# Two of the four column chunks of the output projection as a block of seven products

## The chip, the core and the metric

The kernel runs on one core of a Trainium2 chip. A core has TensorE (PE, matrix products), VectorE (DVE) and ScalarE (ACT) for elementwise work, GpSimd (POOL), SyncE (SP, which issues most transfers) and 16 DMA engines. The metric is the device time of one launch in microseconds; the kernel before takes 2113.49 us, the median of three runs.

## What is computed

One decoder layer for 256 rows of width 2048, in float32: a SwiGLU feed-forward block, a token mixer (block-sparse attention and a convolution in parallel, merged by gates), a second feed-forward block, and a layer norm behind each. The change concerns the end of the mixer:

```
def token_mixer(h, w_in, ..., w_attn_out, w_out):
    ...
    merged = jax.nn.sigmoid(ga) * y_attn + jax.nn.sigmoid(gc) * y_conv
    return merged @ w_out                      # 256 x 2048 by 2048 x 2048
...
    h = layer_norm(DN_ALPHA * h + mix, ln2_g[l], ln2_b[l])
```

## The kernel before

**Arithmetic.** A float32 product is made of three PE products of a faster type: each factor is split into a high part (a rounded copy, made by ACT) and a low part (the rest, made by DVE), and hi x hi, hi x lo and lo x hi are summed in a bank of the accumulator. For a block of weights that means: a transfer lands it, ACT writes the high part, DVE the low part, then PE multiplies. A weight in this chain is either a *unit* (128x1024, half a megabyte, names raw, w_hi, w_lo, lines 767, 1315 and 2197 to 2199) or a *group* (128x2048, one megabyte: four blocks of 128 rows by 512 columns; names g_raw, g_hi, g_lo, lines 817, 1338 and 2259 to 2261).

**Where each way is used.** The feed-forward blocks and the mixer's input projection use groups. For pairs of column chunks, U and G, they use seven products instead of eight (Strassen's scheme in Winograd's form): the 256 x K factor is cut into four blocks (two row tiles, two halves of K), sums S1 to S4 of these are formed once (line 1540), and for each pair of chunks sums T1 to T4 of weight groups take the place of some of the weights. Such a sum is made by DVE (line 1346) or by a transfer from HBM that adds onto what lies in SBUF, which POOL issues (line 2102). The results share four banks X, Y, Z, W; what two results have in common is copied from bank to bank by ACT (fork, line 899).

**The output projection before** uses units: four column chunks of 512, each with 8 units of 2 blocks. A loop over chunks (rows_out) does for each chunk the units 0 to 3 for row tile 0, the same for row tile 1, then units 4 to 7 likewise; DVE adds each finished tile to the residual rows (line 1570) and takes the statistics for the norm (lines 1660, 1663). The last chunk does all of row tile 0 first, so that the norm of tile 0 (lines 1570 to 1605) runs beside PE's work on tile 1. The factor is the merged rows, turned by PE (turn_merged, line 2245) and split into oT_hi and oT_lo. Ahead of it stands the convolution's output projection, behind it the norm and the second feed-forward block.

**What sets the order.** Everything is written out by hand. Each engine runs its own list in order, and an instruction that waits holds back all behind it. Loads are issued by SP in one list; a load into a slot of g_raw waits until the low part of the slot's former content is made. Groups go round a ring of four split buffers (RING), so a split on ACT also waits until PE has used the group four places earlier.

## Time and profile before

| | |
|---|---|
| median of the runs (three: 2112.50 to 2113.76 us) | 2113.49 us |
| span of the profiled execution | 2109.5 us |
| PE busy, matmuls and transposes | 2095.7 us (99%), 9386 |
| DVE busy | 1877.2 us (89%) |
| ACT busy | 1402.9 us (67%) |
| POOL busy | 216.7 us (10%) |
| output projection, in the span | 1339.1 to 1427.9 us |

The span is the time from the first to the last instruction of the one profiled execution; the runs' times lie 4.0 us above it. All positions below are microseconds from the span's start. The busy time of PE counts each matmul by its length in the pipeline, with overlaps merged; the pace of PE is the distance between starts.

### The profile page before, as it was taken

How to read it: one execution, taken by the hardware profiler on the slowest of the kernel's cores; microseconds unless marked ns; L12 is line 12 of the kernel's file. 1: busy time of each engine (PE TensorE's matmuls, PEld its weight loads, DVE VectorE, ACT ScalarE, POOL GpSimd, SP SyncE). 2: the span in 40 equal slices, each digit the busy share in tenths (PEclk: the TensorE clock that was granted, in tenths of full speed). 3: DMA queues.
4: the chain of work that ended last, by engine and by line, in shares of the span. 5: the costliest groups of instructions: out<-in, count | busy, mean ns of one | idle time of the engine just before them, and what ended most of it. 6: DMA issues, size and time to landing. Idle time of an engine off the chain costs nothing.

```text
span 2109.5 us, 23778 instructions
## 1 busy us (share of the span) xinstructions
PE 2095.7 (99%) x9386; PEld 1734.6 (82%) x9386; DVE 1877.2 (89%) x1420; ACT 1402.9 (67%) x1313; POOL 216.7 (10%) x345
## 2 busy tenths in 40 slices
PE   9999999999999999999999999999999999999998
PEld 7888888888888888888888888888888888888886
DVE  7899999999996889999999986659899999999996
ACT  6677777777775546766676445335677777777773
POOL 0111111101110001011100000000111111100110
PEclk9999999999999999999999999999999999999999
DMA  9798988888985759998898556755788988899892
GB/s 369 253 295 260 279 270 266 291 300 277 289 279 231 276 158 311 299 269 270 304 301 262 212 185 240 260 178 200 244 294 255 282 272 267 290 302 278 288 285 113
DMA packets 92397, 556.65 MB, mean 264 GB/s; under 512 B 13056, under 2 KB 13440, under 8 KB 35200
## 3 DMA queue, kind: packets, MB, share of 16 engines
q1 hardware_dynamic: 68544, 437.69, 54.7%
q0 software_dynamic: 23744, 117.46, 25.8%
q8 instruction: 74, 1.21, 0.2%
q14 instruction: 35, 0.29, 0.0%
HBM read 534.13 MB, written 20.97 MB: 263 GB/s over the span
## 4 chain that ended last, share of the span: by engine, by line
PE 88%; DVE 8%; DMA 2%; ACT 1%; issue 1%; SPq 0%; DVEq 0%; ACTq 0%
PE acc L2259 14%; PE acc L2261 14%; PE acc L2260 14%; PE tb L2259 12%; PE tb L2261 12%; PE tb L2260 12%; PE acc L2197 3%; PE acc L2199 3%; PE acc L2198 3%; DVE g_lo L1338 3%; DVE cacc L1777 3%; DMA g_raw<-in_groups 1%; PE tb L2245 1%; DVE w_lo L1315 1%; DVE g_raw L1346 1%
## 5 line engine op out<-in xcount | busy, mean ns | idle before, releaser
L1338 DVE TENSOR_TENSOR g_lo<-g_raw,g_hi 128x2048 fp32r<-128x2048 f32 x506 | 1147.6, 2286 | 120.4 <-ACT g_hi L817 119.8
L817 ACT ACTIVATE g_hi<-g_raw 128x2048 fp32r<-128x2048 f32 x506 | 964.4, 1916 | 319.8 <-DVE g_raw L1346 121.5
L2259 PE MATMUL acc<-g_hi,xF_hi 128*128 128x512 f32 x1184 | 464.3, 392 | 0.6 <-ACT acc L899 0.6
L2261 PE MATMUL acc<-g_hi,xF_lo 128*128 128x512 f32 x1184 | 461.1, 389 | 0.0
L2260 PE MATMUL acc<-g_lo,xF_hi 128*128 128x512 f32 x1184 | 460.7, 389 | 0.0
L2259 PE MATMUL tb<-g_hi,xF_hi 128*128 128x512 f32 x760 | 296.3, 390 | 0.3 <-DVE g_lo L1338 0.2
L2261 PE MATMUL tb<-g_hi,xF_lo 128*128 128x512 f32 x760 | 295.7, 389 | 0.0
L2260 PE MATMUL tb<-g_lo,xF_hi 128*128 128x512 f32 x760 | 295.7, 389 | 0.0
L1346 DVE TENSOR_TENSOR g_raw<-g_raw,g_raw 128x2048 f32<-128x2048 f32 x120 | 274.3, 2286 | 1.3
L2259 PEld LDWEIGHTS acc<-g_hi,xF_hi 128*128 128x128 f32 x1184 | 222.3, 188 | 46.8 <-ACT acc L899 1.0
L2261 PEld LDWEIGHTS acc<-g_hi,xF_lo 128*128 128x128 f32 x1184 | 222.2, 188 | 46.8
L2260 PEld LDWEIGHTS acc<-g_lo,xF_hi 128*128 128x128 f32 x1184 | 222.4, 188 | 45.1
L2259 PEld LDWEIGHTS tb<-g_hi,xF_hi 128*128 128x128 f32 x760 | 142.7, 188 | 30.4 <-issue 1.1
L2261 PEld LDWEIGHTS tb<-g_hi,xF_lo 128*128 128x128 f32 x760 | 142.6, 188 | 29.8
L2102 POOL DMA_DIRECT2D g_raw<-in_groups x80 | 72.5, 941 | 918.8 <-DVE g_lo L1338 870.6
L2260 PEld LDWEIGHTS tb<-g_lo,xF_hi 128*128 128x128 f32 x760 | 142.7, 188 | 29.4
L767 ACT ACTIVATE w_hi<-raw 128x1024 fp32r<-128x1024 f32 x80 | 84.7, 1062 | 105.0 <-DMA raw<-in_stream 65.4
L2259 PE MATMUL tb<-g_hi,hT_hi 128*128 128x512 f32 x384 | 149.8, 390 | 0.0
L2261 PE MATMUL tb<-g_hi,hT_lo 128*128 128x512 f32 x384 | 149.4, 389 | 0.0
L2260 PE MATMUL tb<-g_lo,hT_hi 128*128 128x512 f32 x384 | 149.4, 389 | 0.0
L2259 PE MATMUL acc<-g_hi,hT_hi 128*128 128x512 f32 x320 | 124.7, 390 | 0.0
L2261 PE MATMUL acc<-g_hi,hT_lo 128*128 128x512 f32 x320 | 124.5, 389 | 0.0
(180 smaller groups left out, 2307.7 us busy)
## 6 DMA issues: line engine op xcount, KB each, us to landing
g_raw<-in_groups SPq DMA_DIRECT2D x356, 1024.0 KB, 7.2
g_raw<-in_groups POOLq DMA_DIRECT2D x80, 1024.0 KB, 8.6
raw<-in_stream SPq DMA_DIRECT2D x80, 512.0 KB, 4.5
bounce<-h_sq POOLq DMA_DIRECT2D x40, 256.0 KB, 5.5
h_in<-bounce POOLq DMA_DIRECT2D x160, 64.0 KB, 2.6
ln_gb<-in_ln SPq DMA_DIRECT2D x6, 1024.0 KB, 6.6
g_raw<-in_groups SPq DMA_DIRECT2D x6, 512.0 KB, 9.7
res<-in_x_rows SPq DMA_DIRECT2D x1, 2048.0 KB, 16.6
```

Of the source, the lines that this page charges most:

```text
L767: act.activation(w_hi[:, seg.split(j)], raw[:, seg.raw(j)], ACT.Copy).then_inc(hi_ready, 1)
L817: act.activation(g_hi[:, n % RING], source[:], ACT.Copy).then_inc(g_hi_ready, 1)
L1338: dve.tensor_tensor(g_lo[:, n % RING], source[:], f32(g_hi[:, n % RING]), ALU.subtract).then_inc(g_lo_ready, 1)
L1346: dve.tensor_tensor(out[:], a[:], b[:], ALU.add).then_inc(t_ready, 1)
L1777: ins = dve.scalar_tensor_tensor(out=rows if j == TAPS - 1 else cacc[:, k], in0=rows, scalar=w, in1=cacc[:, k], op0=ALU.mult, op1=ALU.add)
L2102: pool.dma_start(out=source(f, b, onto)[:].rearrange("p k n -> p (k n)"), in_=groups[k], accum_op=ALU.add).then_inc(ready, 16)
L2197: pe.matmul(out_ap, x[0][:, k, rows], w_hi[:, s, cols], start=begin, stop=False)
L2198: pe.matmul(out_ap, x[0][:, k, rows], w_lo[:, s, cols], start=False, stop=False)
L2199: return pe.matmul(out_ap, x[1][:, k, rows], w_hi[:, s, cols], start=False, stop=end)
L2259: pe.matmul(bank, x_hi_ap, g_hi[:, n % RING, blk], start=begin, stop=False, skip_group_check=True)
L2260: pe.matmul(bank, x_hi_ap, g_lo[:, n % RING, blk], start=False, stop=False, skip_group_check=True)
L2261: return pe.matmul(bank, x_lo_ap, g_hi[:, n % RING, blk], start=False, stop=end, skip_group_check=True)
```

## The change

The weights of the output projection are loaded as groups. Column chunks 0 and 3 stay plain (groups a0 to a3 and b0 to b3). Chunks 1 (U) and 2 (G) become one block of seven products P1 to P7, each in two halves a and b of four matmul blocks. Its loads are qa, qb, ga, gb (chunk G) and ra, rb, ua, ub (chunk U). PE's order is the table OUT: P1a and P1b stand between a1 and a2. Six of the eight sums of weights are made by accumulating transfers (T1: q + r, T3: r + u, T4: q + g, for a and b), two by DVE (T2: q + u). The four factor sums are made by DVE and split by ACT and DVE. The loads of the norm's constants and of the second feed-forward block's first groups move behind the block's loads in SP's list, and SP's slots for these change. Core of the diff:

```diff
+OUT = ("a0", "a1", "P1a", "P1b", "a2", "a3", "P2a", "P2b", "P5a", "P5b", "P6a", "P3a", "P6b", "P3b", "P7a", "P7b", "P4a", "P4b",
+       "b0", "b1", "b2", "b3")
+OUT_LOADS = {"a0": "a0", "a1": "a1", "qa": "P4a", "qb": "P4b", "a2": "a2", "ra": "P7a", "rb": "P7b", "a3": "a3", "ga": "P2a",
+             "gb": "P2b", "ua": "P3a", "ub": "P3b", "b0": "b0", "b1": "b1", "b2": "b2", "b3": "b3"}
+OUT_SUMS = ("T2a", "T2b")
+OUT_FACTORS = (S1, S2, S4, S3)
+OUT_PLAIN = (0, 3)
+OUT_U, OUT_G = 1, 2
...
-            load_once(mix_out)
-
-            for j in range(mix_out.n):
-                load(mix_out, 1, j)
-            sp.wait_ge(tr_full, t_ln2)
+            slot_free(KO, 4)
+            load_group(KO)
+            sp.wait_ge(tr_full, t_convt + 4)
+            load_group(KO + 1)
+            load_group(KO + 2)
+            sp.wait_ge(lo_ready, UNITS - 2)
+            load_group(KO + 3)
+            sp.wait_ge(lo_ready, UNITS)
+            load_group(KO + 4)
+            for k in range(KO + 5, K1):
+                if k in G.behind_conv:
+                    sp.wait_ge(unit_used, UNITS)
+                load_group(k)
+            sp.wait_ge(g_used, G.at["out", 0, "P7b"] + 1)
             load_gb(1, ln_gb[1])
-            for k in range(K1, K1 + 2):
+            for k in range(K1, K2):
+                if k in G.behind_out:
+                    sp.wait_ge(g_used, N1)
                 load_group(k)
-            loads(mix_out, 2)
-            sp.wait_ge(unit_used, mix_out.unit(ND - 1, 0))
-            sp.wait_ge(lo_ready, mix_out.unit(ND - 1, UD))
-            for k in range(K1 + 2, K1 + 4):
-                load_group(k)
-            sp.wait_ge(unit_used, mix_out.unit(ND - 1, UD))
-            load_ffn(1, K1 + 4, K2)
...
+            def out_pair():
+
+                f, g = "out", 0
+                split_out("a2")
+                out_factor_hi(0)
+                split_out("a3")
+                out_factor_hi(1)
+                fork(f, g, acc[:, BY], acc[:, BX], "P1b")
+                split_loaded(f, g, "P2a", "ga")
+                out_factor_hi(2)
+                split_loaded(f, g, "P2b", "gb")
+                out_factor_hi(3)
+                act.wait_ge(t1a_ready, 16)
+                split(f, g, "P5a", "qa")
+                act.wait_ge(t1b_ready, fulls(f, g) - 16 * NG)
+                split(f, g, "P5b", "qb")
+                split_sum(f, g, "P6a", "qa", "T2a")
+                split_loaded(f, g, "P3a", "ua")
+                split_sum(f, g, "P6b", "qb", "T2b")
+                act.wait_ge(acc_out[1], 2 * (u1_end + 1))
+                fork(f, g, acc[:, BZ], acc[:, BW], "P5b")
+                split_loaded(f, g, "P3b", "ub")
+                act.wait_ge(t3a_ready, 16 * BLOCKS)
+                split(f, g, "P7a", "ra")
+                act.wait_ge(t3b_ready, fulls(f, g))
+                split(f, g, "P7b", "rb")
+                save_out(0, "P6b")
+                act.wait_ge(t4a_ready, fulls(f, g))
+                split(f, g, "P4a", "qa")
+                act.wait_ge(t4b_ready, 16 * (BLOCKS + 1))
+                split(f, g, "P4b", "qb")
+                save_out(1, "P7b")
...
+            def plain_rows(m, t):
+
+                if m and t == 0:
+                    dve.wait_ge(out_full, 1)
+                else:
+                    dve.wait_ge(g_used, G.at["out", 0, ("a3", "b3")[m]] + 1)
+                cols = slice(OUT_PLAIN[m] * COLS, (OUT_PLAIN[m] + 1) * COLS)
+                dve.scalar_tensor_tensor(out=res[:, t, cols], in0=res[:, t, cols], scalar=ALPHA, in1=acc[:, 2 + t],
+                                         op0=ALU.mult, op1=ALU.add).then_inc(acc_out[1], 1)
...
+            def out_pair():
+
+                f, g = "out", 0
+                qa, qb, ua, ub = (source(f, g, name) for name in ("qa", "qb", "ua", "ub"))
+                lo_group(f, g, "P1b", "qb")
+                out_factor_sum(0)
+                lo_out("a2")
+                out_factor_sum(1)
+                lo_out("a3")
+                out_factor_sum(2)
+                out_factor_lo(0)
+                lo_group(f, g, "P2a", "ga")
+                out_factor_lo(1)
+                out_factor_sum(3)
+                lo_group(f, g, "P2b", "gb")
+                out_factor_lo(2)
+                lo_group(f, g, "P5a", "qa")
+                load_done(f, g, "ua")
+                split_done(f, g, "P5a")
+                add(qa, qa, ua)
+                plain_rows(0, 0)
+                plain_rows(0, 1)
+                lo_group(f, g, "P5b", "qb")
+                lo_group(f, g, "P6a", "qa")
+                load_done(f, g, "ub")
+                split_done(f, g, "P5b")
+                add(qb, qb, ub)
+                lo_group(f, g, "P3a", "ua")
+                lo_group(f, g, "P6b", "qb")
+                out_factor_lo(3)
+                lo_group(f, g, "P3b", "ub")
+                lo_group(f, g, "P7a", "ra")
+                lo_group(f, g, "P7b", "rb")
+                g_rows(0)
+                lo_group(f, g, "P4a", "qa")
+                u_rows(0)
+                lo_group(f, g, "P4b", "qb")
+                u_rows(1)
...
+            out_pair()
+            lo_out("b0")
+            for t in range(TT):
+                plain_stats(0, t)
+            lo_out("b1")
+            g_rows(1)
+            lo_out("b2")
+            for n, t, c in ((1, 0, OUT_G), (2, 0, OUT_U), (3, 1, OUT_U)):
+                pair_stats(n, t, c)
+            lo_out("b3")
+            pair_stats(4, 1, OUT_G)
...
+            def out_sums():
+
+                f, g = "out", 0
+                pool.wait_ge(g_lo_ready, lo_count(G.at[f, g, "P1a"]))
+                add_from_hbm(f, g, "qa", "ra", t1a_ready)
+                pool.wait_ge(g_lo_ready, lo_count(G.at[f, g, "P1b"]))
+                add_from_hbm(f, g, "qb", "rb", t1b_ready)
+                for name, onto, ready in (("ra", "ua", t3a_ready), ("rb", "ub", t3b_ready)):
+                    k = G.load_at[f, g, name]
+                    pool.wait_ge(g_loaded[slot_of[k]], 16 * (slot_count[k] - sum(slot_of[h] == slot_of[k] for h in range(PARTED))))
+                    add_from_hbm(f, g, name, onto, ready)
+                pool.wait_ge(g_lo_ready, lo_count(G.at[f, g, "P6a"]))
+                add_from_hbm(f, g, "qa", "ga", t4a_ready)
+                pool.wait_ge(g_lo_ready, lo_count(G.at[f, g, "P6b"]))
+                add_from_hbm(f, g, "qb", "gb", t4b_ready)
+
+            out_sums()
...
+            def out_pair():
+
+                f, g = "out", 0
+                X, Y, Z, W = (acc[:, bank] for bank in (BX, BY, BZ, BW))
+                made = 7 + 4 * factors(f)
+                pe.wait_ge(lhs_lo, b_merge + 4)
+                out_plain(0, 0, True, False)
+                out_plain(1, 0, False, False)
+                turn_merged(ND - 1)
+                out_plain(0, 1, True, False)
+                out_plain(1, 1, False, False)
+                pe.wait_ge(acc_out[0], 2 * u0_mix)
+                out_product("P1a", X, A11, 0, begin=True)
+                out_product("P1b", X, A11, 1)
+                pe.wait_ge(lhs_lo, b_ln2)
+                for t in range(TT):
+                    out_plain(2, t, False, False)
+                    out_plain(3, t, False, True)
+                wait_fork(f, g, 0)
+                out_product("P2a", Y, A12, 0)
+                out_product("P2b", Y, A12, 1)
+                pe.wait_ge(x_lo, made + 1)
+                pe.wait_ge(acc_out[1], 2 * (u1_end + 1))
+                out_product("P5a", W, S1, 0, begin=True)
+                out_product("P5b", W, S1, 1)
+                pe.wait_ge(x_lo, made + 2)
+                out_product("P6a", X, S2, 0)
+                wait_fork(f, g, 1)
+                pe.wait_ge(x_lo, made + 3)
+                out_product("P3a", Z, S4, 0)
+                out_product("P6b", X, S2, 1)
+                out_product("P3b", Z, S4, 1)
+                wait_fork(f, g, 2)
+                pe.wait_ge(x_lo, made + 4)
+                out_product("P7a", X, S3, 0)
+                out_product("P7b", X, S3, 1)
+                wait_fork(f, g, 3)
+                out_product("P4a", X, A22, 0)
+                out_product("P4b", X, A22, 1)
...
+            def last_out():
+
+                n = G.at["out", 0, "b0"]
+                pe.wait_ge(out_rows, 1 + TT)
+                for t in range(TT):
+                    for p in range(PIECES):
+                        if t == 0:
+                            wait_lo(pe, n + p)
+                        hi_part, lo_part = out_piece(p, t)
+                        for blk in range(GK):
+                            mm = mm3(acc[:, 2 + t], hi_part[:, blk], lo_part[:, blk], n + p, blk, p == 0 and blk == 0,
+                                     p == PIECES - 1 and blk == GK - 1)
+                        if t == 1:
+                            mm.then_inc(g_used, 1)
+                            if p >= 2:
+                                turn_piece(p - 2, 10, b_ln2)
+                        elif p == PIECES - 1:
+                            mm.then_inc(out_full, 1)
...
```

In the rows below, g_raw_6N is slot N of g_raw (g_raw_70 is slot 10), acc is one of the four banks, and each row is one instruction or a repeated one, with the semaphores it waits for.

DVE, the output projection. Before, the rows ahead of the loop over chunks (w_lo is a unit's low part, oT_lo the low part of the turned rows):

```order
L1315 TENSOR_TENSOR w_lo<-raw,w_hi 128x1024 [waits hi_ready] x4
L1326 TENSOR_TENSOR oT_lo<-tb,oT_hi 128x4x128 [waits lhs_hi] x2
L2014 TENSOR_TENSOR sig_c<-sig_c,acc 128x512 [waits tile0_full]
L2014 TENSOR_TENSOR sig_c<-sig_c,acc 128x512 [waits unit_used]
L2017 TENSOR_TENSOR sig_a<-sig_a,sig_c 128x512 [waits acc_out0] x2
L1315 TENSOR_TENSOR w_lo<-raw,w_hi 128x1024 [waits hi_ready] x4
L1326 TENSOR_TENSOR oT_lo<-tb,oT_hi 128x4x128 [waits lhs_hi] x2
```

After, from the low part of P2a to that of P3a:

```order
L1446 TENSOR_TENSOR g_lo<-g_raw_69,g_hi 128x2048 [waits g_hi_ready]
L1668 TENSOR_TENSOR xF_lo<-raw_F,xF_hi 128x1024 [waits x_hi]
L1662 TENSOR_TENSOR raw_F<-raw_F 128x1024 [waits s_made]
L1446 TENSOR_TENSOR g_lo<-g_raw_61,g_hi 128x2048 [waits g_hi_ready]
L1668 TENSOR_TENSOR xF_lo<-raw_F,xF_hi 128x1024 [waits x_hi]
L1446 TENSOR_TENSOR g_lo<-g_raw_70,g_hi 128x2048 [waits g_hi_ready]
L1454 TENSOR_TENSOR g_raw_70<-g_raw_70,g_raw_68 128x2048 [waits g_lo_ready,g_loaded8]
L1770 SCALAR_TENSOR_TENSOR res<-res,acc 128x512 [waits g_used] x2
L1446 TENSOR_TENSOR g_lo<-g_raw_60,g_hi 128x2048 [waits g_hi_ready]
L1446 TENSOR_TENSOR g_lo<-g_raw_70,g_hi 128x2048 [waits g_hi_ready]
L1454 TENSOR_TENSOR g_raw_60<-g_raw_60,g_raw_69 128x2048 [waits g_lo_ready,g_loaded9]
L1446 TENSOR_TENSOR g_lo<-g_raw_68,g_hi 128x2048 [waits g_hi_ready]
```

The loop's unit low parts with two row operations for each chunk have become a straight list, in which the two row operations of chunk 0 (L1770) stand behind the low part of P5a and the sum T2a (L1454).

ACT, the same place. Before, the last rows ahead of the loop over chunks:

```order
L778 ACTIVATE oT_hi<-tb 128x4x128 [waits tr_full] x2
L767 ACTIVATE w_hi<-raw 128x1024 [waits raw_loaded0,unit_used]
L767 ACTIVATE w_hi<-raw 128x1024 [waits raw_loaded1,unit_used]
L767 ACTIVATE w_hi<-raw 128x1024 [waits raw_loaded2,unit_used]
L767 ACTIVATE w_hi<-raw 128x1024 [waits raw_loaded3,unit_used]
L778 ACTIVATE oT_hi<-tb 128x4x128 [waits tr_full] x2
```

After, from P6a's split to that of P4b, with the three copies between banks or into act_sb (L956):

```order
L874 ACTIVATE g_hi<-g_raw_70 128x2048 [waits g_used,t_ready]
L874 ACTIVATE g_hi<-g_raw_68 128x2048 [waits g_used,g_loaded8]
L874 ACTIVATE g_hi<-g_raw_60 128x2048 [waits g_used,t_ready]
L956 ACTIVATE acc<-acc 128x512 [waits g_used,acc_out1]
L874 ACTIVATE g_hi<-g_raw_69 128x2048 [waits g_used,g_loaded9]
L874 ACTIVATE g_hi<-g_raw_64 128x2048 [waits g_used,t3a_ready]
L874 ACTIVATE g_hi<-g_raw_65 128x2048 [waits g_used,t3b_ready]
L956 ACTIVATE act_sb<-acc 128x512 [waits g_used]
L874 ACTIVATE g_hi<-g_raw_70 128x2048 [waits g_used,t4a_ready]
L874 ACTIVATE g_hi<-g_raw_60 128x2048 [waits g_used,t4b_ready]
L956 ACTIVATE act_sb<-acc 128x512 [waits g_used]
```

Splits that waited for a load and a free unit now wait for sums (t_ready, t3a_ready to t4b_ready), and copies of banks stand between them.

SP, the loads behind the residual's second half. Before:

```order
L730 DMA res<-kept 128x2048
L627 DMA raw<-in_stream 128x1024 [waits lo_ready] x16
L640 DMA ln_gb<-in_ln 128x2048 [waits tr_full]
L640 DMA ln_gb<-in_ln 128x2048
L647 DMA g_raw_64<-in_groups 128x2048
L647 DMA g_raw_65<-in_groups 128x2048
L630 UNCONDITIONAL_BRANCH
```

After:

```order
L700 DMA g_raw_64<-in_groups 128x2048 [waits g_lo_ready]
L700 DMA g_raw_65<-in_groups 128x2048 [waits tr_full]
L700 DMA g_raw_70<-in_groups 128x2048
L700 DMA g_raw_60<-in_groups 128x2048 [waits lo_ready]
L700 DMA g_raw_61<-in_groups 128x2048 [waits lo_ready]
L700 DMA g_raw_64<-in_groups 128x2048 [waits g_lo_ready]
L700 DMA g_raw_65<-in_groups 128x2048 [waits g_lo_ready]
L700 DMA g_raw_68<-in_groups 128x2048 [waits unit_used]
L700 DMA g_raw_69<-in_groups 128x2048 [waits unit_used]
L700 DMA g_raw_61<-in_groups 128x2048 [waits g_lo_ready]
L700 DMA g_raw_68<-in_groups 128x2048 [waits g_lo_ready]
```

The group loads stand in one list; gb is the one into g_raw_61 behind the two that wait for unit_used (a3 and ga are those two), and it waits for a low part (of a2, the former content of that slot). On POOL the six accumulating transfers (out_sums above) stand between two pairs of the norms' line 2122.

## Rows read from the trace of the kernel before

**Rows 1.** The page: span, busy time by engine, and the chain that ended last.

```profile
span 2109.5 us, 23778 instructions
...
PE 2095.7 (99%) x9386; PEld 1734.6 (82%) x9386; DVE 1877.2 (89%) x1420; ACT 1402.9 (67%) x1313; POOL 216.7 (10%) x345
...
PE 88%; DVE 8%; DMA 2%; ACT 1%; issue 1%; SPq 0%; DVEq 0%; ACTq 0%
```

**Rows 2.** Waits of PE: who was waited for, us in total, times, longest.

```profile
PE tb L2323 <- DVE zeros L1683: 1.5, 1, 1.5
...
PE acc L2197 <- DVE sig_a L1950: 0.7, 1, 0.7
PE acc L2259 <- ACT acc L899: 0.6, 1, 0.6
```

**Rows 3.** Window, output projection: length, busy PE, PEld, DVE, ACT, POOL, clock, DMA.

```profile
1338.60:1427.80 89.20, 89.20 (x402) 73.86 (x401) 53.75 (x56) 34.37 (x32) 0.55 (x1) 1.00 0.59 212
```

**Rows 4.** Timeline of DVE, output projection: start, length, operation, idle before.

```profile
1345.86 1.29 DVE L1326 TENSOR_TENSOR oT_lo<-tb,oT_hi 128x512 fp32r<-128x512 f32 x2
...
1416.43 0.69 DVE L1570 SCALAR_TENSOR_TENSOR res<-res,acc 128x512 f32<-128x512 f32 x1 [4.72 <-PE acc L2199]
```

**Rows 5.** Timeline of PE, the output projection from its start.

```profile
1339.14 0.39 PE L2197 MATMUL acc<-w_hi,oT_hi 128*128 128x512 f32 x1
1339.37 0.39 PE L2198 MATMUL acc<-w_lo,oT_hi 128*128 128x512 f32 x1
...
1344.59 1.04 PE L2245 MATMUL tb<-ident,sig_a 128*128 128x128 f32 x8
1345.38 0.47 PE L2197 MATMUL acc<-w_hi,oT_hi 128*128 128x512 f32 x1
1345.70 0.39 PE L2198 MATMUL acc<-w_lo,oT_hi 128*128 128x512 f32 x1
```

**Rows 6.** Groups by line (busy us, mean ns), then timelines.

```profile
L1338 DVE TENSOR_TENSOR g_lo<-g_raw,g_hi 128x2048 fp32r<-128x2048 f32 x506 | 1147.6, 2286 | 120.4 <-ACT g_hi L817 119.8
L817 ACT ACTIVATE g_hi<-g_raw 128x2048 fp32r<-128x2048 f32 x506 | 964.4, 1916 | 319.8 <-DVE g_raw L1346 121.5
...
L1315 DVE TENSOR_TENSOR w_lo<-raw,w_hi 128x1024 fp32r<-128x1024 f32 x80 | 95.4, 1223 | 16.6 <-ACT w_hi L767 16.3
...
859.69 8.89 DVE L1338 TENSOR_TENSOR g_lo<-g_raw,g_hi 128x2048 fp32r<-128x2048 f32 x4
...
1341.15 4.62 DVE L1315 TENSOR_TENSOR w_lo<-raw,w_hi 128x1024 fp32r<-128x1024 f32 x4
...
847.47 3.71 ACT L817 ACTIVATE g_hi<-g_raw 128x2048 fp32r<-128x2048 f32 x2
```

**Rows 7.** DMA issues, 1439 to 1450: count, KB each, median us to landing.

```profile
g_raw<-in_groups SPq DMA_DIRECT2D x3, 1024.0 KB, 5.0
```

**Rows 8.** DMA issues, 840 to 872, loads (SPq) beside accumulating transfers (POOLq).

```profile
g_raw<-in_groups SPq DMA_DIRECT2D x5, 1024.0 KB, 12.2
g_raw<-in_groups POOLq DMA_DIRECT2D x4, 1024.0 KB, 15.7
```

**Rows 9.** All accumulating transfers, L2102: us from issue to landing.

```profile
DMA to landing us min/median/max: 7.8/8.6/20.9
```

**Rows 10.** Timelines of ACT and PE in the mixing block, near 793.

```profile
791.76 1.92 ACT L817 ACTIVATE g_hi<-g_raw 128x2048 fp32r<-128x2048 f32 x1 [4.07 <-DVE g_raw L1346]
793.59 0.58 ACT L899 ACTIVATE acc<-acc 128x512 f32<-128x512 f32 x1
...
793.22 0.39 PE L2261 MATMUL acc<-g_hi,xF_lo 128*128 128x512 f32 x1
794.22 0.50 PE L2259 MATMUL acc<-g_hi,xF_hi 128*128 128x512 f32 x1 [0.61 <-ACT acc L899]
```

**Rows 11.** PE at the program's start: timeline, then the group of that line.

```profile
1.47 3.78 PE L2323 MATMUL tb<-zeros 128*128 128x512 f32 x8 [1.47 <-DVE zeros L1683]
...
L2323 PE MATMUL tb<-zeros 128*128 128x512 f32 x10 | 4.6, 645 | 1.5 <-DVE zeros L1683 1.5
```

More of the change, by code:

```diff
@@ L66 @@
 MIX_SLOTS = 8
+ALL_SLOTS = 11
 RING = 4
@@ L660, in load_ffn @@
                     load_group(k)
-            KM, KG, K1, K2 = (G.begin[x][1] for x in ("mix", "gates", 1, "end"))
+            KM, KG, KO, K1, K2 = (G.begin[x][1] for x in ("mix", "gates", "out", 1, "end"))
             sp.dma_start(x_stage[:, 0:2], xT[:, 0:2]).then_inc(x_loaded[0], 16)
```

226 lines of the change are left out of this document (155 added, 71 removed).

## Prediction

> **What bounds the kernel now.** I read the page's head first: TensorE (PE) is busy 2095.7 of 2109.5 us and holds 88% of the chain that ended last [rows 1]. The waits by engine come next. PE hardly waits at all: 1.5 us at the start, and otherwise nothing over 0.8 [rows 2]. So the time is the number of matmuls times their spacing, and a change pays only if it takes matmuls out and adds no wait on PE. Then the stretches. The output projection runs from 1339.1 to 1427.9, PE is busy in all of it, VectorE (DVE) in 53.75 us and ScalarE (ACT) in 34.37 of the 89.2 [rows 3]. What DVE has left there is what the change spends. The timeline of PE gives the spacing: 1339.14 to 1339.37 is 0.227 us for a 128x512 matmul (the printed 0.39 is its length in the pipeline), eight transposes take 0.79 (1344.59 to 1345.38), and the first matmul behind them is followed after 0.32, so a restart costs 0.1 [rows 5].
>
> **What is removed.** The projection has 4 column chunks x 16 blocks x 2 row tiles x 3 matmuls = 384. Afterwards the two plain chunks keep 192 and the block has 14 half products x 12 = 168, in all 360. 24 x 0.2267 = **5.44 us** come off PE, and this is all that the change can win: 0.26% of the time.
>
> **What is added on DVE, the engine that now counts.** The spacing of a 128x2048 op there is (8.89 - 2.29) / 3 = 2.20, of a 128x1024 op (4.62 - 1.23) / 3 = 1.13, of a 128x512 op 0.60 (1.29 for two); of a 128x2048 split on ACT 1.80 (3.71 for two), and a copy between banks takes 0.58 [rows 4, 6, 10]. DVE had 32 low parts x 1.13 = 36 us. It gets 22 low parts and 2 weight sums (24 x 2.20 = 53), 4 factor sums and 4 factor low parts (8 x 1.13 = 9), and the row work, with one op more for each row tile of the U chunk. That fills its slack; what matters is where its queue stands when PE needs a part. I go through PE's products in order. The anchors are PE's start at 1339.14 [rows 5] and the end of the last turned low parts on DVE, 1345.86 + 2 x 0.60 = 1347.1 [rows 4]; both stay, as all ahead of them is unchanged.
>
> *P5a.* PE reaches the end of P2b after 144 matmuls, 0.8 of transposes and 0.1: 1339.14 + 32.6 + 0.9 = 1372.7. P5a begins in the bank that holds chunk 0's rows, so it waits for both plain_rows, and these stand on DVE behind the low parts of P2b and P5a and the sum T2a. DVE is through with all ahead of the low part of P2b at 1347.1 + 4 low parts (8.8) + 4 factor sums and 2 factor low parts (6.8) + 0.4 for a wait = 1363.1. From there it needs 3 x 2.20 + 1.13 + 2 x 0.60 + 0.2 = 9.1 to the second plain_rows: 1372.2, in time by half a microsecond. But P2b's weights (load gb) reuse the slot of a2, so the load is issued when the low part of a2 is done: 1347.1 + 2.20 + 1.13 + 2.20 + 0.1 = 1352.8. By then three of the six accumulating transfers are out (t1b behind the low part of P1b at about 1349.8, t3a and t3b right behind, at the 0.9 us an issue takes on POOL). A load by itself lands after 5.0 us [rows 7]; among four accumulating transfers five loads took 12.2 in the median [rows 8]. So gb lands between 1357.8 and 1365.0. With the first, the wait is 0. With the second, ACT's split ends at 1366.9, DVE has stood for 3.8 us, and plain_rows end at 1376.0: 3.3 us of wait. The rows at 840 are the same mixture (loads from one queue, accumulates from the other), so I take **3.0** of that; the first accumulate is already some way through when gb starts. Behind the waiting instruction on DVE are all later low parts, so nothing catches up.
>
> A rule speaks for the other end: the Trainium skill, "DMA: Bandwidth & Descriptors" (section "Anatomy of one DMA — SWDGE"), fits a transfer issued by GpSimd with about 2.0 us plus its bytes over 436e3 per us, which makes an estimate of 4.4 us for 1 MB. By it the accumulates would be gone soon and the sum below would be that of the first rival. The trace disagrees: the quickest of 80 accumulates took 7.8 us, the median 8.6 [rows 9].
>
> *P3a.* It waits for the copy of bank W to bank Z (fork f1) on ACT. This stands behind the split of P6b, which waits for the sum T2b. From the release of P5a, PE needs 3 x 2.72 = 8.2 to P3a; DVE needs 3 x 2.20 for two low parts and T2b, then ACT 1.8 and 0.58: 9.1 with the hand-overs. So **0.9**. The mixing block shows the same chain: a split that waited 4.07 for a sum, the copy behind it, and PE standing from 793.22 to 794.22 instead of 0.23 [rows 10]. This one doesn't hang on DMA.
>
> *P4a.* It overwrites bank X, which ACT saves after P7b with nothing between. Drain of the last matmul (0.2), copy 0.58 and hand-over make 0.9, near the 0.8 of [rows 10]. If t4b lands late the save stands behind the split of P4b, up to 0.9 more (t4a and t4b go out 6.6 us apart, and b1 and b2 are loaded beside them). I take **1.2**.
>
> *b1 to b3, row tile 0.* From the release of P5a to the low part of b0 DVE has 11 x 2.20 + 1.13 + 5 x 0.60 + 0.4 = 28.7 us, PE 10 x 2.72 + 0.9 + 1.2 = 29.3: b0 is just in time. Then DVE has 3 low parts with six small ops between (two stats, one row op, three stats): 6.6 + 3.6 = 10.2, PE 3 x 2.72 = 8.2. So **2.0**, mostly ahead of b3.
>
> Four restarts at 0.1 add **0.4**. Edits at nothing: the two ln loads and the FFN's first loads move behind the block; they are needed at 1416 to 1421, and DVE's chain of the norm, which began at 1416.43 with row tile 0's end [rows 4], is covered by row tile 1's 48 matmuls as before (if the loads came later than that, each us would show). POOL's six accumulates stand ahead of the norm's rstd, which it needs 20 us later. SP now waits in order on DVE's low parts; all it holds back is the next load, counted above for gb.
>
> **Sum.** -5.44 + 3.0 + 0.9 + 1.2 + 2.0 + 0.4 = **+2.1 us**. Against the profiled execution's own span of 2109.5 that is 2111.6; the median of the runs, 2113.5, lies 4.0 above that span [rows 1], so 2115.6.
>
> **Rivals.**
> 1. *Loads not held up.* If the 16 engines serve gb before the accumulates, P5a waits 0 and P4a 0.9: -5.44 + 0.9 + 0.9 + 2.0 + 0.3 = -1.3, 2112.2. For it: 5.0 us for a load by itself, and t3a, t3b have just been issued and may not have started. Against it: the 12.2 of [rows 8].
> 2. *Full gain.* -5.4 and 2108.1, if DVE and ACT cover everything. Against it: 0.9, 0.9 and 2.0 come from order and spacing alone. To be over 0.2% faster at most 1.2 us of waits may be left.
> 3. *Slower: accumulates pile up.* In the stretch at 840 the accumulates themselves took 15.7 us [rows 8]. If gb gets less than half of the engines and lands 3 us later than 1365, at 1368, the low part of P2b ends at 1372.1, past P2b's start (1370.0): PE waits 2.1 there and 4.2 at P5a; if t4b takes 12 to 13 us instead of 8 to 9, P4a waits 3 to 4. -5.44 + 2.1 + 4.2 + 0.9 + 1.2 + 2.0 + 0.4 = +5.4, 2118.9; with a late t4b up to 2121. It decides from a landing of gb some 15 us after its issue. For it: three accumulates are ahead of gb, not one or two. Against it: the loads at 840 had four beside them and took 12.2.
> 4. *The clock falls in P5a's wait.* The granted clock is 1.00 in the projection [rows 3], and no row shows PE idle for 3 us after its start. The first matmuls, behind 1.5 us without work, stand 0.45 apart ((3.78 - 0.64) / 7 [rows 11]), twice the later spacing; some 4 us at that pace would cost 2 us on top of the forecast: 2117.6. The Trainium skill, "TensorE: Matmul & The Clock Gate" (section "Part 1: The HAM clock gate"), has the array fall to 1.2 GHz after idling, and no run here shows whether so short a wait does it.
>
> **How the numbers follow.** Forecast (2114 to 2117.5): 0.45, as the mixture of loads and accumulates is what the trace shows. Rival 1 (2110.5 to 2114): 0.28. Rival 2: 0.07. Rival 3: 0.16. Rival 4: 0.04. The predicted time is 2115.6. The range runs from 2110.6 to 2119.2 and leaves out rival 2 and the upper part of rival 3. About 0.2%, 4.2 us, is what a measurement can tell from no change: faster than 2109.3 is rival 2 with the edge of rival 1, 0.09; slower than 2117.7 is rival 3 and part of 4 and of the forecast's upper edge, 0.21; within, 0.70.
>
> **What the changed profile would show.** PE's waits: P5a for a row op on DVE (3 us; near 0 means rival 1), P3a for a copy on ACT (0.9), P4a for a copy on ACT (0.9 to 1.8), and the fourth piece of the last chunk for a low part on DVE (1.4). DVE: a gap of 3 us ahead of the low part of P2b, behind an ACT split that waits for DMA. The row op of the last chunk's row tile 0 at about 1418.5 instead of 1416.43. Granted clock 1.00 throughout. The forecast is wrong if gb lands within 9 us of its issue, if PE waits at P2b as well, or if the stages after the projection begin with a wait that they didn't have.

## The result, and the profile after

The changed kernel took 2117.78 us in the median of seven runs (2115.10 to 2121.97), the kernel before 2112.50 beside it (seven runs, 2110.44 to 2114.42). The ratio is 1.0027, with a 95% interval of 1.0018 to 1.0036: slower by 3.8 to 7.6 us. A later comparison of the same two kernels, with more runs, gave 1.0012 (1.0002 to 1.0021). Both say slower; how much is known only to within some 4 us, and the second profile of the changed kernel, below, shows part of the reason.

The page of the changed kernel: span, and busy time by engine. They answer to [rows 1].

```profile
span 2113.3 us, 23576 instructions
...
PE 2092.7 (99%) x9362; PEld 1730.3 (82%) x9362; DVE 1903.1 (90%) x1422; ACT 1417.1 (67%) x1315; POOL 221.9 (10%) x351
```

24 matmuls are gone (9362 for 9386), PE has 3 us less work, and the span is 3.8 us longer. So PE stands where it did not. The waits of PE, which answer to [rows 2]:

```profile
PE acc L2465 <- DVE res L1770: 3.9, 1, 3.9
...
PE tb L2746 <- issue: 1.5, 1, 1.5
PE acc L2465 <- DVE g_lo L1446: 1.3, 2, 1.0
PE acc L2465 <- ACT act_sb L956: 0.7, 1, 0.7
```

A wait of 3.9 us for the row op of chunk 0 (L1770) is new, and so are 1.3 us for low parts and 0.7 us for a save of a bank (act_sb, L956). The line with L2746 (1.5 us; 0.8 before) lies ahead of the projection, in code that the change leaves alone; it comes back below.

The timeline of PE: the projection's first matmul, the wait, what follows it, and the last matmul (start, length, operation, idle before). The first row answers to [rows 5].

```profile
1339.48 0.39 PE L2465 MATMUL acc<-g_hi,oT_hi 128*128 128x512 f32 x1
...
1372.91 0.39 PE L2467 MATMUL acc<-g_hi,oT_lo 128*128 128x512 f32 x1
1377.25 0.76 PE L2465 MATMUL acc<-g_hi,xF_hi 128*128 128x512 f32 x1 [3.94 <-DVE res L1770]
1377.81 0.63 PE L2466 MATMUL acc<-g_lo,xF_hi 128*128 128x512 f32 x1
1378.23 0.63 PE L2467 MATMUL acc<-g_hi,xF_lo 128*128 128x512 f32 x1
...
1380.64 0.39 PE L2467 MATMUL acc<-g_hi,xF_lo 128*128 128x512 f32 x1
...
1431.13 0.39 PE L2467 MATMUL acc<-g_hi,oT_lo 128*128 128x512 f32 x1
```

The last matmul of the projection in the kernel before:

```profile
1427.38 0.39 PE L2199 MATMUL acc<-w_hi,oT_lo 128*128 128x512 f32 x1
```

From first to last matmul the projection took 88.23 us before (1339.14 to 1427.38, from the times before rounding) and 1431.13 - 1339.48 = 91.65 now, 3.4 us more. From its last matmul to the end of PE's last matmul in the program both kernels need the same 672.3 us. The rest of the difference of the spans (0.3 us) had arisen before the projection began. Two things stand in these rows. PE starts P5a 4.33 us after the last matmul of P2b instead of 0.23. And the matmuls behind it are 0.43 us apart, not 0.23, until 1380.64. The windows of PE (length, busy time and instructions, granted clock, DMA share, GB/s) say what that is:

```profile
1372.90:1380.60 7.70, 3.75 (x10) 0.78 0.57 242
1380.60:1400.00 19.40, 19.40 (x87) 1.00 0.87 226
```

The clock granted was 0.78 of full in the stretch with the wait and the slow matmuls, and 1.00 behind it; at 0.43 us a matmul PE ran at the lower of its two levels, 1.2 GHz. This costs 1.4 us (seven times 0.20), beside 4.1 for the wait.

ACT and DVE show where the wait comes from. First ACT, then DVE, which answers to [rows 4]; in brackets the idle time and what ended it.

```profile
1365.97 1.92 ACT L874 ACTIVATE g_hi<-g_raw 128x2048 fp32r<-128x2048 f32 x1 [5.70 <-DMA g_raw<-in_groups]
...
1385.61 0.58 ACT L956 ACTIVATE acc<-acc 128x512 f32<-128x512 f32 x1
...
1399.07 1.92 ACT L874 ACTIVATE g_hi<-g_raw 128x2048 fp32r<-128x2048 f32 x1 [4.02 <-DMA g_raw<-in_groups]
1400.89 0.57 ACT L956 ACTIVATE act_sb<-acc 128x512 f32<-128x512 f32 x1
```

```profile
1367.92 2.29 DVE L1446 TENSOR_TENSOR g_lo<-g_raw,g_hi 128x2048 fp32r<-128x2048 f32 x1 [4.00 <-ACT g_hi L874]
...
1375.87 1.28 DVE L1770 SCALAR_TENSOR_TENSOR res<-res,acc 128x512 f32<-128x512 f32 x2
...
1420.18 0.69 DVE L1770 SCALAR_TENSOR_TENSOR res<-res,acc 128x512 f32<-128x512 f32 x1 [2.50 <-PE acc L2467]
```

ACT's split of P2b (1365.97) had waited 5.70 us for a load, DVE's low part of it (1367.92) 4.00 us for that split; behind it stand two further low parts (of a factor sum and of P5a) and T2a, and then the two row ops at 1375.87 that P5a needs. The load itself, issued at 1353.1, in the DMA issues (KB, us to landing):

```profile
g_raw<-in_groups SPq DMA_DIRECT2D x1, 1024.0 KB, 12.9
```

It is gb, and it took 12.9 us, where a load by itself takes 5.0 [rows 7]. The wait at 1399.07 is of the same kind: it is for t4b, the second of the last two accumulating transfers; the save of X at 1400.89 stands behind that split.

### The profile page after: what moved, and what is told of

It is laid out like the page before. It is cut to its first block, busy times and chain, and to the rows that moved or that the text cites. A ratio compares the mean times of both kernels' runs of the same rounds, so it can differ in the third digit from the quotient of the medians.

```text
span 2113.3 us, 23576 instructions
## 1 busy us (share of the span) xinstructions
PE 2092.7 (99%) x9362; PEld 1730.3 (82%) x9362; DVE 1903.1 (90%) x1422; ACT 1417.1 (67%) x1315; POOL 221.9 (10%) x351
## 4 chain that ended last, share of the span: by engine, by line
PE 87%; DVE 8%; DMA 2%; ACT 1%; issue 1%; SPq 0%; DVEq 0%; ACTq 0%
PE acc L2465 15%; PE acc L2467 15%; PE acc L2466 15%; PE tb L2465 12%; PE tb L2467 12%; PE tb L2466 12%; DVE g_lo L1446 3%; DVE cacc L1921 3%; DMA g_raw<-in_groups 2%; PE acc L2412 1%; PE acc L2413 1%; PE acc L2414 1%; PE tb L2451 1%; DVE w_lo L1423 1%; DVE g_raw L1454 1%
## 5 line engine op out<-in xcount | busy, mean ns | idle before, releaser
L1446 DVE TENSOR_TENSOR g_lo<-g_raw,g_hi 128x2048 fp32r<-128x2048 f32 x528 | 1197.5, 2285 | 128.2 <-ACT g_hi L874 127.7
L874 ACT ACTIVATE g_hi<-g_raw 128x2048 fp32r<-128x2048 f32 x528 | 1005.8, 1915 | 337.5 <-DVE g_raw L1454 128.1
L2465 PE MATMUL acc<-g_hi,xF_hi 128*128 128x512 f32 x1216 | 477.6, 393 | 4.6 <-DVE res L1770 3.9
L2467 PE MATMUL acc<-g_hi,xF_lo 128*128 128x512 f32 x1216 | 474.1, 390 | 0.0
L2466 PE MATMUL acc<-g_lo,xF_hi 128*128 128x512 f32 x1216 | 473.7, 390 | 0.0
L1454 DVE TENSOR_TENSOR g_raw<-g_raw,g_raw 128x2048 f32<-128x2048 f32 x122 | 278.8, 2285 | 1.4
L2465 PEld LDWEIGHTS acc<-g_hi,xF_hi 128*128 128x128 f32 x1216 | 228.7, 188 | 52.3 <-issue 4.3
L2467 PEld LDWEIGHTS acc<-g_hi,xF_lo 128*128 128x128 f32 x1216 | 228.6, 188 | 48.0
L2466 PEld LDWEIGHTS acc<-g_lo,xF_hi 128*128 128x128 f32 x1216 | 228.9, 188 | 46.6
L2297 POOL DMA_DIRECT2D g_raw<-in_groups x86 | 77.7, 948 | 1043.6 <-DVE g_lo L1446 995.7
L2466 PE MATMUL acc<-g_lo,hT_hi 128*128 128x512 f32 x320 | 124.5, 389 | 0.0
```

Of the source, the lines that this page charges most:

```text
L874: act.activation(g_hi[:, n % RING], source[:], ACT.Copy).then_inc(g_hi_ready, 1)
L1446: dve.tensor_tensor(g_lo[:, n % RING], source[:], f32(g_hi[:, n % RING]), ALU.subtract).then_inc(g_lo_ready, 1)
L1454: dve.tensor_tensor(out[:], a[:], b[:], ALU.add).then_inc(t_ready, 1)
L2297: pool.dma_start(out=source(f, b, onto)[:].rearrange("p k n -> p (k n)"), in_=groups[k], accum_op=ALU.add).then_inc(ready, 16)
L2465: pe.matmul(bank, x_hi_ap, g_hi[:, n % RING, blk], start=begin, stop=False, skip_group_check=True)
L2466: pe.matmul(bank, x_hi_ap, g_lo[:, n % RING, blk], start=False, stop=False, skip_group_check=True)
```

## The experiments

A figure called *stage* is the time from the first to the last matmul of the projection in that kernel's trace; this is the part of the program that the edits touch. In each of the twelve traces, PE needs 672.2 to 672.4 us from there to the end of its last matmul. A wait given *beyond the spacing* is the distance between the starts of two neighbouring matmuls less the usual 0.23 us; the profile's own number for the same wait, the idle time, is some 0.16 us less.

| kernel | stage, us | ratio to the kernel before (95%) |
|---|---|---|
| before | 88.23 | |
| changed | 91.65 | 1.0027 (1.0018 to 1.0036) |
| changed, second profile | 92.27 | 1.0012 (1.0002 to 1.0021) |
| e1_loads | 89.09 | 0.9997 (0.9988 to 1.0007) |
| e2_t3late | 88.24 | one run |
| e3_fill | 93.46 | one run |
| e4_stats | 90.66 | one run |
| e7_forks | 89.02 | one run |
| e8_all | 86.50 | 0.9989 (0.9980 to 0.9998) |
| e9_p2b | 87.43 | 0.9992 (0.9983 to 1.0001) |
| e10_split_first | 85.33 | 0.9986 (0.9977 to 0.9995) |
| e11_p2b_factor | 84.27 | 0.9982 (0.9973 to 0.9991) |

### e1_loads: is it the late load?

```diff
-OUT_LOADS = {"a0": "a0", "a1": "a1", "qa": "P4a", "qb": "P4b", "a2": "a2", "ra": "P7a", "rb": "P7b", "a3": "a3", "ga": "P2a",
-             "gb": "P2b", "ua": "P3a", "ub": "P3b", "b0": "b0", "b1": "b1", "b2": "b2", "b3": "b3"}
+OUT_LOADS = {"a0": "a0", "a1": "a1", "qa": "P4a", "qb": "P4b", "a2": "a2", "a3": "a3", "ga": "P2a", "gb": "P2b", "ua": "P3a",
+             "ra": "P7a", "rb": "P7b", "ub": "P3b", "b0": "b0", "b1": "b1", "b2": "b2", "b3": "b3"}
```

> The changed kernel with another order of loads: a3, ga, gb and ua go out before ra and rb, so that gb has a slot at about 1340 and is no longer behind accumulating transfers. Theory (the late gb makes the wait at P5a, and the wait makes the clock fall): ACT's split of P2b doesn't wait for DMA, DVE has no gap of 4 us ahead of the low part of P2b, PE waits under 0.5 us at P5a, no matmuls 0.43 us apart follow; about 0.9 us of wait appears at P3a (the copy behind P6b's split), 0.9 to 1 stays at P4a and 1.5 to 2 at the last chunk's pieces. Sum against the kernel before: -5.4 + 0.9 + 0.9 + 2.0 + 0.3 = -1.3 us. Rival (DVE is full, so that the 4 us turn up at later products): the P5a wait goes, but the waits from P3a on grow by 3 to 5 us, and the time stays 3 to 5 us above before.

gb and ua went out at about 1340 (two loads, median 5.9 us):

```profile
g_raw<-in_groups SPq DMA_DIRECT2D x2, 1024.0 KB, 5.9
```

DVE ran from P1b's low part to P5a's without a gap over 0.7 us, P5a started 0.34 us after the last matmul of P2b (0.11 over the usual spacing), and there were no slow matmuls. The mechanism is thus confirmed. The waits that remain:

```profile
PE acc L2465 <- ACT act_sb L956: 2.9, 1, 2.9
...
PE acc L2465 <- ACT acc L956: 1.2, 2, 0.6
```

P3a's wait for the copy has appeared: 0.76 us beyond the spacing, against 0.9 forecast. (The acc line counts it with the one of [rows 10].) But P4a's wait grew from 0.9 to 3.06. ACT shows why:

```profile
1396.52 1.91 ACT L874 ACTIVATE g_hi<-g_raw 128x2048 fp32r<-128x2048 f32 x1 [6.17 <-DMA g_raw<-in_groups]
1398.33 0.58 ACT L956 ACTIVATE act_sb<-acc 128x512 f32<-128x512 f32 x1
```

t4b landed 12.1 us after its issue, and the save stood behind the split that waits for it. So 5.5 us came off at P5a and the slow matmuls behind it, and 3.0 came back at P3a and P4a. The stage is 0.9 us above the kernel before, where I had expected 1.3 below; the times say no difference (0.9997). The rival was right that part of the gain turns up later, wrong that DVE is the reason: it was a transfer and an order on ACT.

### e2_t3late: the queue of accumulates, or the slot?

```diff
                 add_from_hbm(f, g, "qb", "rb", t1b_ready)
+                pool.wait_ge(g_lo_ready, lo_count(G.at[f, g, "P2b"]))
                 for name, onto, ready in (("ra", "ua", t3a_ready), ("rb", "ub", t3b_ready)):
```

> The changed kernel with one edit: POOL issues the two accumulates t3a and t3b only when the low part of P2b is made; gb is issued where it was. Theory (gb is held up by the accumulates queued beside it): gb lands within 10 us of its issue, instead of 12.85, P5a waits under 1 us, and the clock doesn't fall. Rival (gb is late because its slot comes free late): gb lands as late as in the changed kernel and P5a still waits 4 us. Either way t3a and t3b land some 15 us later than now, which leaves them about in time for P7.

gb was issued at the same point, and landed after 7.7 us:

```profile
g_raw<-in_groups SPq DMA_DIRECT2D x1, 1024.0 KB, 7.7
```

P5a waited 0.1 us beyond the spacing, with no slow matmuls. So it is the accumulates t3a and t3b beside gb that make it late, not its slot: 12.9 us with them, 7.7 with t1b alone (t1a had landed before gb was issued in both traces). The stage, 88.24, is that of the kernel before. Behind the wait at P4a (2.0 us of idle time, 2.2 beyond the spacing) the slow matmuls came here as well:

```profile
1399.75 0.50 PE L2466 MATMUL acc<-g_hi,oT_hi 128*128 128x512 f32 x1 [2.02 <-ACT act_sb L956]
...
1400.55 0.57 PE L2466 MATMUL acc<-g_hi,oT_hi 128*128 128x512 f32 x1
1400.91 0.63 PE L2467 MATMUL acc<-g_lo,oT_hi 128*128 128x512 f32 x1
```

### e3_fill: does standing lower the clock?

```diff
                 pe.wait_ge(x_lo, made + 1)
+                for _ in range(16):
+                    pe.matmul(tb[:, 0], oT_hi[:, 0, 0:P], oT_hi[:, 0:2].rearrange("p b n -> p (b n)"), start=True, stop=True,
+                              skip_group_check=True)
                 pe.wait_ge(acc_out[1], 2 * (u1_end + 1))
```

> The changed kernel with 16 matmuls of 512 columns that nobody reads, 3.6 us of work, ahead of the wait at P5a; the wait itself stays. Theory (PE standing for 4 us is what lowers the clock): no matmuls 0.43 us apart behind the wait, P5a's first matmul starts when it did, and the 1.6 us return; 0.5 to 0.9 of it is lost again at P3a, where the copy is late, so the span is 0.5 to 1.5 us shorter. Rival (the clock falls there for another reason): the slow matmuls remain and the span is the same.

```profile
1374.84 3.79 PE L2931 MATMUL tb<-oT_hi 128*128 128x512 f32 x16
1379.37 0.50 PE L2465 MATMUL acc<-g_hi,xF_hi 128*128 128x512 f32 x1 [0.73 <-DVE res L1770]
1379.70 0.40 PE L2466 MATMUL acc<-g_lo,xF_hi 128*128 128x512 f32 x1
```

With the wait filled, 0.73 us of it left, the matmuls behind it run 0.23 us apart: it is the standing that lowers the clock. But the stage became longer, 93.46, by 1.8 us, not shorter. P3a's 0.75 came back, and P4a waited 2.99 for t4b instead of 0.9. Counted from the projection's start, t4b was issued 0.4 us later, as ua landed late and held DVE up (0.86 us ahead of T2a), and it took 12.0 us where it took 10.6 in the first profile; nothing shows that the added matmuls made it slower. The rows of the changed kernel itself show what the clock costs there: the save of X (1400.89) stood behind the split that waits for t4b, and P7b's last matmul, started at 1400.39, was hardly earlier. With the full clock PE would have come there earlier and waited for the same split. By these rows the 1.4 us were nearly free. What the expectation says of the clock holds, its price does not.

### e4_stats: the last chunk

```diff
             lo_out("b0")
-            for t in range(TT):
-                plain_stats(0, t)
             lo_out("b1")
             g_rows(1)
             lo_out("b2")
-            for n, t, c in ((1, 0, OUT_G), (2, 0, OUT_U), (3, 1, OUT_U)):
-                pair_stats(n, t, c)
+            plain_stats(0, 0)
             lo_out("b3")
+            pair_stats(1, 0, OUT_G)
+            pair_stats(2, 0, OUT_U)
+            plain_stats(0, 1)
+            pair_stats(3, 1, OUT_U)
             pair_stats(4, 1, OUT_G)
```

> The changed kernel with five of the six statistics of DVE moved behind the low part of b3 (one stays ahead of it). Theory (the last chunk's waits are small ops in DVE's queue between the low parts): the waits of b1 (0.5) and b3 (1.1) with their restarts, 1.8 us, go, and the span is 1 to 2 us shorter; the norm behind it has the slack. Rival (DVE is bound by the low parts themselves, or the norm becomes late): b3 waits as before or the second feed-forward block starts with a wait, no gain.

No wait is left at b1 and b3: the 1.6 us of waits and 0.2 of restarts are gone as expected, and the second feed-forward block begins without one. The stage is only 1.0 us shorter, since the other wait was longer in this execution:

```profile
PE acc L2466 <- DVE res L1770: 4.4, 1, 4.4
```

It was 4.5 us in place of 4.1 beyond the spacing, with eleven matmuls 0.43 us apart behind it in place of seven.

### after_again: a second profile of the changed kernel

> The changed kernel itself, unedited, with a second profile. It tells how far the waits differ from execution to execution: in the first profile the projection's first to last matmul took 91.65 us against 88.23 before, 3.4 us more, while the timed runs are 5 to 6 us longer. Theory (the landing of gb and of t4b among the other transfers varies, and the clock falls in some waits only): gb again 12 to 14 us after its issue, 4 to 5 us of wait at P5a, and a wait at P4a between 0.9 (t4b in time) and 3; stage 91 to 94. Rival (the time is lost outside the projection): the stage again at 91.6 and another place that differs from before.

```profile
PE acc L2465 <- DVE res L1770: 3.9, 1, 3.9
PE tb L2746 <- issue: 3.9, 2, 2.3
```

gb landed after 13.5 us, P5a waited 4.1 beyond the spacing, with twelve slow matmuls behind it: stage 92.27. But the span was 2118.0, 4.7 us longer than in the first profile, and 4.1 of that lie ahead of the projection, which began at 1343.55. The line with L2746 is part of it: 3.9 us here, 1.5 in the first profile. The clock is another part: it fell behind the longer of these two waits, as the windows of PE around 920 say, and in the first profile it fell nowhere ahead of the projection.

```profile
915.00:919.80 4.80, 2.45 (x14) 1.00 0.91 185
919.80:923.20 3.40, 3.40 (x14) 0.50 1.06 219
```

So the rival holds in part as well. Over the twelve traces the first matmul of the projection lies between 1338.15 and 1343.55, behind matmuls that no edit touches. The timed runs contain this spread, which is larger than the 3 us in question.

### e7_forks: two copies on ACT

Early loads as in e1_loads, and:

```diff
-                split_sum(f, g, "P6b", "qb", "T2b")
                 fork(f, g, acc[:, BZ], acc[:, BW], "P5b")
+                split_sum(f, g, "P6b", "qb", "T2b")
...
+                save_out(1, "P7b")
                 split(f, g, "P4b", "qb")
-                save_out(1, "P7b")
```

> The early loads of e1_loads, and on ACT two copies moved: the copy of W to Z ahead of P6b's split, the save of X ahead of P4b's split. Theory: the 0.76 at P3a goes (the sum T2b comes after P5b's end anyway), the wait at P4a falls from 3.06 to 0.9 (drain, copy, hand-over), and what t4b's late landing costs turns up at P4b instead, 0 to 1.5 us. Stage (first to last matmul of the projection) 87 to 88 against 89.1 in e1_loads. Rival (the copies wait for PE, not for the splits): both waits as in e1_loads.

```profile
PE acc L2465 <- DVE g_lo L1446: 3.5, 5, 1.1
...
PE acc L2465 <- ACT act_sb L956: 0.7, 1, 0.7
```

P4a fell to 0.85 beyond the spacing. At P3a only 0.17 of the 0.76 went: it waits no longer for the copy, but 0.59 for its own low part, which stands on DVE behind two others and T2b. P4b waited 1.28 for its split (t4b landed after 11.2 us), b0 0.82 behind that. The stage, 89.02, is that of e1_loads, where 87 to 88 was expected. The copies were what PE waited for, and moving them gained nothing while t4b was late and DVE full: the delay moved one place down.

### e8_all: t4b in time, and DVE's small ops moved

e7_forks, and: the loads of b2 and b3 wait for t4b; u_rows(1), g_rows(0), g_rows(1) and five statistics move behind b0's, b2's and b3's low parts; the last chunk's row tile t waits for u_rows(t) alone.

```diff
+                if k == G.load_at["out", 0, "b2"]:
+                    sp.wait_ge(t4b_ready, 16 * (BLOCKS + 1))
...
-                pe.wait_ge(out_rows, 1 + TT)
                 for t in range(TT):
+                    pe.wait_ge(out_rows, t + 1)
```

> e7_forks, and the row ops and statistics that nobody waits for moved behind the last low parts on DVE, and the loads of b2 and b3 issued when t4b has landed. Theory: t4b lands within 10 us of its issue; the waits left are P4a's 0.9 and at most 1 us at P4b, b0 or b3; the stage takes 83.8 to 85 us against 88.2 before, and the time is 3 to 4.4 us below before, 2108.5 to 2110, ratio 0.998 to 0.9985. Rival (DVE is full: any op moved comes back as a wait on the next low part, or the norm behind begins later): stage 86 to 88, within 1 us of e1_loads.

```profile
PE acc L2468 <- DVE g_lo L1448: 1.5, 2, 1.1
...
PE acc L2468 <- ACT act_sb L958: 0.7, 1, 0.7
```

t4b landed 9.3 us after its issue. The stage fell to 86.50, less than expected (83.8 to 85), and the time below that of before (0.9989). The waits of b0 to b3 are down to 0.23. What I had not seen is P4b's 1.28: with t4b early, its split stood behind the save, which waits for PE.

### e10_split_first: the order on ACT undone

e8_all without its second move on ACT:

```diff
-                save_out(1, "P7b")
                 act.wait_ge(t4b_ready, 16 * (BLOCKS + 1))
                 split(f, g, "P4b", "qb")
+                save_out(1, "P7b")
```

> e8_all with the split of P4b back ahead of the save of X, as in the changed kernel. In e8_all the loads held back let t4b land at 1394.9, but the split of P4b then stood behind the save, which waits for PE until 1397.2, and P4b waited 1.28 us. Theory (whichever of the two is ready first has to stand first; with t4b early that is the split): the wait at P4b goes, P4a keeps its 0.85, the stage takes 85.0 to 85.5 us against 86.5 in e8_all and 88.2 before; ratio to before 0.9985. Rival (t4b lands too late in most executions, so that the split ahead of the save makes P4a wait instead): P4a waits 1.5 to 3, stage 86.5 or more.

```profile
PE acc L2468 <- ACT act_sb L958: 1.3, 1, 1.3
...
PE acc L2468 <- DVE g_lo L1448: 0.4, 1, 0.4
```

P4b's wait is gone, P4a's is 1.45 beyond the spacing. Stage 85.33, as expected; P4a was a little longer than I said.

### e9_p2b and e11_p2b_factor: work for PE beside the save

```diff
-                out_product("P2b", Y, A12, 1)
...
                 out_product("P7b", X, S3, 1)
+                out_product("P2b", Y, A12, 1)
                 wait_fork(f, g, 3)
```

In the lists of ACT and DVE the split and the low part of P2b move with it.

> e8_all with P2b moved from ahead of P5a to between P7b and P4a, so that PE has work while ACT saves X. Theory: P4a's 0.9 goes; P5a comes 2.7 us earlier for PE and 2.2 earlier for DVE, so it waits about 0.5; stage 83 to 84.5, 4 to 5 us below before, near the whole 5.4 us. Rival (DVE has no slack at P5a): P5a waits 1 to 2 us and the stage is as long as in e8_all or longer.

P4a's wait went, but P5a waited 2.52 us beyond the spacing, with eight slow matmuls and part of a ninth behind it. The stage, 87.43, missed the expected 83 to 84.5 and is longer than that of e8_all, as the rival had it; the interval of the ratio includes no change. ACT and DVE:

```profile
1364.95 1.06 ACT L1351 ACTIVATE xF_hi<-raw_F 128x1024 fp32r<-128x1024 f32 x1 [3.69 <-DVE raw_F L1664]
```

```profile
1367.85 2.29 DVE L1448 TENSOR_TENSOR g_lo<-g_raw,g_hi 128x2048 fp32r<-128x2048 f32 x1 [1.79 <-ACT g_hi L876]
```

The high part of the fourth factor sum waited 3.69 us on ACT, and P5a's split, already possible, stood behind it. e11_p2b_factor moves this high part behind P5b's split (and takes e10's order of split and save):

```diff
-                out_factor_hi(3)
                 act.wait_ge(t1a_ready, 16)
                 split(f, g, "P5a", "qa")
                 act.wait_ge(t1b_ready, fulls(f, g) - 16 * NG)
                 split(f, g, "P5b", "qb")
+                out_factor_hi(3)
```

> P2b between P7b and P4a as in e9_p2b, the split of P4b ahead of the save of X as in e10, and the high part of the fourth factor sum moved on ACT behind P5b's split. In e9_p2b this high part waited 3.69 us for DVE's sum on ACT, the split of P5a stood behind it, DVE stood 1.79 us and PE 2.52 us at P5a, with nine slow matmuls behind that. Theory: P5a waits 0.3 to 0.9 us, no slow matmuls, no wait of PE at P4a; stage 83.3 to 84.5 us, 4 to 5 us below before. Rival (DVE's own work is what is late at P5a): P5a waits 1.5 us or more again, stage 85 to 87.

```profile
PE acc L2468 <- ACT acc L958: 0.6, 1, 0.6
PE acc L2468 <- issue: 0.5, 1, 0.5
PE acc L2468 <- DVE g_lo L1448: 0.4, 1, 0.4
```

The first of these lines is that of [rows 10], the second P5a, the third P3a: P5a waits 0.63 beyond the spacing, P3a 0.56, and no other wait in the projection is over 0.05. The stage is 84.27 us, 4.0 below before, and the time 2109.15 against 2112.47 beside it, ratio 0.9982 (0.9973 to 0.9991). This version is faster than both kernels.

## Why the prediction was right, point by point

Forecast was 2115.6 us, 2.1 above before, in a range of 2110.6 to 2119.2. The median lies in the range and above, not below, the kernel before, as forecast. It was slower by 5.3 us in the first comparison, beyond the 0.2% that I had called within no change and given 0.70; in the second it was within that bound. By the stage in the traces, which leaves out what varies ahead of the projection, it is 3.4 and 4.0.

The time fits better than the difference does. The forecast started from 2113.49 us, and beside the changed kernel the one before took 2112.50. The 4.0 us from span to time are not one cost: every run on record took about 1.8 us more than its own span, so the other 2.2 say that the profiled execution was a quick one. The first median, 2117.78, lies just above the band that the prediction gave the forecast itself (2114 to 2117.5), the second, 2115.91, in it.

| term | forecast, us | first trace | second trace |
|---|---|---|---|
| matmuls removed | -5.4 | -5.4 | -5.4 |
| P2b | 0 | 0.1 | 0.6 |
| P5a | 3.0 | 4.1 | 4.1 |
| slow clock behind it | 0 (rival 4) | 1.4 | 2.5 |
| P3a | 0.9 | 0 | 0 |
| P4a | 1.2 | 0.9 | 0.8 |
| b0 to b3 | 2.0 | 1.7 | 0.9 |
| restarts | 0.4 | 0.4 | 0.4 |
| stage, as measured | +2.1 | +3.4 | +4.0 |

The lines are the excess over 0.227 us between neighbouring matmuls of PE; they add up to the stage within 0.2 us. The sum came near with some luck: in the first trace P2b, P5a and the clock were 2.6 us short and P3a, P4a and the last chunk 1.5 us long. The two are linked, since a PE that is late from P5a waits less at P3a (e3_fill shows it) and at P4a.

- *P5a.* Place, chain and cause were right, and the term was too small: gb issued at 1353.1 (forecast 1352.8), behind three accumulates, landing after 12.9 us; e1 and e2 each took the cause away, and the wait went with it. It was undersized by 1.1 us, because I took 3.0 where the row of loads beside accumulates gave 3.3 and the load was 0.7 us slower than that row. The discount for the first accumulate being under way had no row behind it.
- *The clock.* I gave rival 4 a chance of 0.04, as something besides the forecast. It came on top of it. The wait was sized, and what a wait of that length does to PE was left out of the sum because no row before showed it; the sum should have carried its 1 to 2 us as a bound. The Trainium skill, "TensorE: Matmul & The Clock Gate" (section "Part 1: The HAM clock gate"), says that the array's clock falls when PE idles, and e3_fill agrees: with the wait filled, the clock stayed. Not every wait does it, as e1_loads shows: 2.90 us of idle time, no slow matmuls behind it. The sign "granted clock 1.00 throughout" failed (0.78 behind P5a's wait).
- *P3a.* 0 in the changed kernel: the copy on ACT (1385.61) was done at 1386.2, and PE, slowed behind P5a, came to P3a at 1387.0. In e1_loads and e3_fill, where the clock held, it was 0.76 and 0.75 against 0.9.
- *P4a.* 0.9 in the first trace and 0.8 in the second, and 3.0 in e1 and e3: the term is drain, copy and hand-over, plus whatever t4b is late. The upper end in the sum, 1.8, was too low.
- *b0 to b3.* 1.7 for 2.0; e4_stats took it away with the statistics, as worked out.
- *Rival 1* (loads not held up, 2112.2) is what e1_loads made true, and there 2112.58 against 2112.75 was measured: no difference, 1.1 us less gain than worked out; t4b's late landing (2.1 us more at P4a) is enough for that. *Rival 3* had P2b wait as well; it did so in the second trace, by 0.56, which the prediction also lists as a sign that the forecast is wrong. The 15 us that it names as deciding was too high: its own figures have P2b wait once gb lands more than 13.1 us after its issue (a split of 1.9 and a low part of 2.2 ahead of 1370.0), and in the second trace gb took 13.5.
- The row op of the last chunk's row tile 0 came at 1420.18, against 1416.43 before [rows 4] and 1418.5 forecast: the 1.3 us that the sum lacked, and 0.3 of the later start.
- What stays open: why the first comparison of times gave 5.3 us and the second 3.1, where the stage differs by 3.4 and 4.0 in the traces. The start of the projection moves by up to 5.4 us between executions, which is enough for it. The first profile is of the quickest of the seven runs (2115.10 us, mean granted clock 0.998); the slowest took 2121.97 at 0.996, which points to the clock, but there is no trace of it.

## What to carry to other kernels

On a kernel that is bound by one engine, taking work off it pays only what the rest of the schedule can follow: here 24 matmuls were worth 5.4 us, the waits that the order of the queues made, with the clock behind one of them, cost 8.8, and the same arithmetic with another order of loads, copies, splits and row ops kept 4.0 of the 5.4. Look for loads that go out beside accumulating transfers, and for anything in an in-order queue that waits longer than what stands behind it. After each wait is removed, ask which one was hidden behind it: e1, e3 and e7 each gave back part or all of what they took away.
